# The tail of a hybrid decoder step: where a tile's transposes stand among the products, and the order of combining, gating and norms

## The reference

```python
def _rmsnorm(x, g):
    y = x * rsqrt(mean(x * x, axis=-1) + RMS_EPS)
    return y * g

def _post_mixer(h, mix, p_l, w_out_l, norm_ffn_l, ..., norm_ple_l, pgw, ppw):
    h = h + mix @ w_out_l
    h = h + _hier_moe(_rmsnorm(h, norm_ffn_l), ...)      # each token: 2 of 16 experts, weights w1 and w2
    gate = sigmoid(_rmsnorm(h, norm_ple_l) @ pgw)        # pgw: 1024 x 1024
    return h + gate * (p_l @ ppw)

y_prompt = _rmsnorm(hp, norm_final)                      # 512 x 1024
y_sample = _rmsnorm(hs, norm_final)                      # 8 x 1024
```

## Time and profile before

| | us |
|---|---|
| three runs, median | 1059.52 |
| lowest and highest of them | 1059.48, 1064.51 |
| profiled execution, its own time | 1065.51 |
| span from its first to its last instruction | 1063.3 |

### The profile page before, as it was taken

How to read it: one execution, slowest core, us unless ns; L and a number is a source line. 1 busy time by engine, 2 the same in 40 slices (tenths; PEclk the granted TensorE clock), 3 DMA queues, 4 the chain that set the end, 5 groups by cost and what they waited for, 6 DMA issues and landing times.

```text
span 1063.3 us, 15679 instructions
## 1 busy us (share of the span) xinstructions
PE 935.1 (88%) x6393; PEld 495.7 (47%) x6393; DVE 380.2 (36%) x806; ACT 238.3 (22%) x600; POOL 81.6 (8%) x96
## 2 busy tenths in 40 slices
PE   3996999999999999978978997899998978892996
PEld 3453556654547676665435554443333423341442
DVE  3205645562325747354542125221111111112345
ACT  3116212220123223353212112110000000001335
POOL 1000000000004533000000000100000000002100
PEclk9999999997999989978688999899999989997998
DMA  6454233033246662164603606379999999995101
GB/s 208 178 218 178 31 139 139 4 137 142 79 167 221 235 192 82 42 216 139 198 10 114 259 22 256 127 275 347 378 394 401 402 396 388 407 405 208 41 22 61
DMA packets 72099, 208.76 MB, mean 196 GB/s; under 512 B 15937, under 2 KB 48148, under 8 KB 67548
## 3 DMA queue, kind: packets, MB, share of 16 engines
q1 hardware_dynamic: 57344, 184.73, 46.9%
q0 software_dynamic: 3936, 14.22, 4.0%
q10 hardware_dynamic: 10748, 8.80, 2.6%
HBM read 188.31 MB, written 38.25 MB: 213 GB/s over the span
## 4 chain that ended last, share of the span: by engine, by line
PE 71%; DMA 11%; DVE 10%; ACT 4%; issue 2%; SPq 1%; ACTq 0%; POOL 0%; DVEq 0%; POOLq 0%
PE ps L1930 17%; DMA EXPERT<-in_moe_w_up 9%; PE ps L2354 8%; PE ps L1935 8%; PE ps L2240 6%; PE ps L2460 6%; PE ps L2389 3%; PE ps L2363 3%; PE ps L1965 2%; PE ps L2309 2%; PE ps L2011 1%; PE ps L2092 1%; PE ps L2038 1%; PE ps L1939 1%; PE ps L1914 1%
## 5 line engine op out<-in xcount | busy, mean ns | idle before, releaser
L1930 PE MATMUL ps<-xT,EXPERT 128*128 128x512 f32 x384 | 182.1, 619 | 1.2 <-DVE EXPERT L1263 1.2
L2354 PE MATMUL ps<-EXPERT,aF 128*32 128x512 f32 x1024 | 117.3, 611 | 20.5 <-DMA EXPERT<-in_moe_w_up 12.2
L1935 PE MATMUL ps<-EXPERT,xT 128*128 128x384 f32 (+1 forms) x384 | 121.7, 459 | 1.6 <-ACT EXPERT L917 1.6
L1930 PEld LDWEIGHTS ps<-xT,EXPERT 128*128 128x128 f32 x384 | 71.4, 196 | 79.5 <-issue 75.8
L1935 PEld LDWEIGHTS ps<-EXPERT,xT 128*128 128x128 f32 x384 | 78.8, 238 | 24.6 <-issue 3.5
L2354 PEld LDWEIGHTS ps<-EXPERT,aF 128*32 128x32 f32 x1024 | 34.3, 112 | 99.4 <-issue 81.2
L2460 PE MATMUL ps<-EXPERT 128*128 128x512 f32 x128 | 58.7, 618 | 5.3 <-DVE EXPERT L1891 5.3
L2389 PE MATMUL ps<-EXPERT,dF 128*32 128x512 f32 x512 | 58.2, 595 | 3.3 <-ACT dF L1168 3.3
L2240 PE MATMUL ps<-EXPERT,xT 128*128 128x512 f32 x128 | 60.0, 621 | 1.1 <-ACT xT L1087 1.1
L1843 DVE TENSOR_TENSOR dF<-dF,ps 64x512 f32<-64x512 f32 x16 | 11.0, 690 | 138.6 <-ACT dF L1164 138.6
L1164 ACT ACTIVATE dF<-ps 64x512 f32<-64x512 f32 x16 | 9.4, 590 | 207.4 <-PE ps L2354 207.4
(11 more groups left out here) (439 smaller groups left out, 1234.8 us busy)
## 6 DMA issues: line engine op xcount, KB each, us to landing
EXPERT<-in_moe_w_gate SPq DMA_DIRECT2D x16, 2048.0 KB, 15.9
EXPERT<-in_moe_w_up SPq DMA_DIRECT2D x16, 2048.0 KB, 20.9
EXPERT<-in_moe_w_down SPq DMA_DIRECT2D x16, 2048.0 KB, 21.8
EXPERT<-in_w_in SPq DMA_DIRECT2D x13, 1536.0 KB, 6.6
out_win_sample<-in_cache_win SPq DMA_DIRECT2D x16, 1022.0 KB
aF<-in_cache_k_diff SPq DMA_DIRECT2D x32, 192.0 KB, 2.5
aF<-in_cache_v_diff SPq DMA_DIRECT2D x32, 192.0 KB, 2.5
Yd<-wk ACTq DMA_DIRECT2D x34, 128.0 KB, 9.0
```

The source lines that it names most:

```text
L1930: last = t.matmul(ps[:, u % 2, :], W_[:, c, c0:c0 + w], xT[:, c, 0:SEQ], start=(c == 0), stop=(c == DC - 1))
L1935: last = t.matmul(ps[:, u % 2, 0:w], rows_, W_[:, c, c0:c0 + w], start=(c == 0), stop=(c == DC - 1))
L2354: last = t.matmul(ps[32 * q:32 * q + 32, 2, :], xgT[:, c, 32 * (q % 2):32 * (q % 2) + 32], w[:, c, :], start=(c == 0), stop=(c == DC - 1))
```

## The change

On TensorE, the transposes of tile i + 1 move from behind ple(i) to between its two halves. For tile 4, which has no two halves, `ple` returns before that place, and there is no tile 5.

On VectorE, the loop's body becomes two functions, `combine` (steps 2 and 4) and `gate_columns` (step 6), and tile i + 1 is combined right behind the columns of tile i, ahead of the finish of tile i - 1. The last norm of tile i - 2 and the finish of tile i - 1 change places.

On ScalarE, the rms of tile i + 1 stands ahead of the gate of tile i - 1, and the last rms of tile i - 2 ahead of both.

No operation is added or taken away.

```diff
@@ ScalarE
-            for i in range(T5):
+            def tile_rms(i):
                 act.wait_ge(S_["comb_ok"], i + 1)
                 inv_rms(i, "hn_e")
+
+            tile_rms(0)
+            tile_rms(1)
+            for i in range(1, T5):
                 if i >= 2:
                     act.wait_ge(S_["po_ok"], i - 1)
                     inv_rms(i - 2, "n4_e")
-                if i:
-                    gate(i - 1)
-                    s.preload_act_table_set("natural_log_exp_and_others")
+                if i < NT:
+                    tile_rms(i + 1)
+                gate(i - 1)
+                s.preload_act_table_set("natural_log_exp_and_others")
             gate(NT)
@@ VectorE
-            for i in range(T5):
+            def combine(i):
+
                 r = tile_rows(i)
                 dve.wait_ge(yload[i % 2], 32 * (i // 2 + 1))
...
                 v.tensor_scalar(Ub[i % 3][0:r, :], XM[0:r, i, :], rstd[0:r, i:i + 1], None,
                                 ALU.mult).then_inc(S_["hn_ok"], 1)
+
+            def gate_columns(i):
+
+                r = tile_rows(i)
                 dve.wait_ge(S_["hnt_pe"], i + 1)
                 if i >= 2:
                     dve.wait_ge(S_["pg_pe"], i - 1)
...
                                 f2(gains[:, 16:24], r), ALU.mult).then_inc(S_["hnt_ok"], 1)
+
+            combine(0)
+            for i in range(T5):
+                gate_columns(i)
+                if i < NT:
+                    combine(i + 1)
+                if i >= 2:
+                    last_norm(i - 2)
                 if i:
                     finish(i - 1)
-                if i >= 2:
-                    last_norm(i - 2)
             finish(NT)
@@ TensorE, ple(i)
                 for hf in range(2):
+                    if hf:
+                        columns(i + 1)
                     for c in range(DC):
                         last = t.matmul(ps[0:r, 4 + 2 * (i % 2) + hf, :], hnT[i % 2][:, c, 0:r],
                                         ple_[:, c, hf * 512:(hf + 1) * 512], start=(c == 0), stop=(c == DC - 1))
@@ TensorE
             columns(0)
             for i in range(T5):
                 ple(i)
-                if i < NT:
-                    columns(i + 1)
```

## The result

The changed kernel's median is 1054.03 us over 20 runs, the kernel before's in the same comparison 1059.49 us over 20 runs. The ratio is 0.9933, 95% interval [0.9908, 0.9957]: faster by 0.7%, or 1052.4 us (1049.8 to 1055.0) on the scale of the 1059.52 us given before. The ratio of the two medians given here is 0.9948, or 1054.0 us, which lies inside the range.

What follows compares the result with a forecast made beforehand. The prediction took TensorE's chain of products, transposes and VectorE's copy-out to bound the tail. Gains of 1.48, 3.17 and 0.63 us made 5.28, of which 5.2 reach the end: 1059.52 - 5.2 = 1054.3 us, range 1053.0 to 1059.6.

Steps and rivals of the forecast that it cites:

- The mechanism: TensorE's gate products in the tail: transposes between product halves hide the copy-out; about 5.2 us reach the end.
- The four waits: TensorE's idle time ahead of tiles 1 to 3 and the sample product: 1.31, 1.32, 1.32 and 0.46 us would go.
- the period: TensorE, one tile's products to the next's: 14.61 us in place of 16.20, priced from the w_out stage.
- Tile 3 with the small transposes: TensorE, tile 3 up to the sample product: 14.43 us in place of 15.06, 0.63 us gained.
- ScalarE's table at the end: ScalarE, sample tile's sigmoid: table in 3.81 us after the sample product's start, last by about 0.1 us.
- the scatter: Whole-kernel time: half a microsecond or so allowed around gains of 5.41 to 4.41 us.
- B: Whole-kernel median: the time doesn't show, since runs lie 5.0 us apart outside the tail; 1059.3 us, chance 18%.
- A: Gate products: only the idle time goes, pieces start up as now; 4.4 us, 1055.1 us, within the forecast's 73%.
- C: Middle of products: VectorE and ScalarE become the bound, transposes wait for scaled rows; no change, 1059.5 us, chance 4%.
- D: Middle of tiles 0 to 3: the clock falls at the transposes; 12.9 us, 1067.2 us, 0.7% slower, chance 5%.
- D's price for a fall: Middle of a tile's products: 2.54 us for six slow passes and 0.90 us for eight transposes, 3.4 us.

Runs made afterwards that it cites:

- after_again: The changed kernel, unedited, measured again against the kernel before: ratio 0.9968 [0.9943, 0.9992], tail 80.11 us.
- after_third: The changed kernel, unedited, measured once more against the kernel before: ratio 0.9946 [0.9908, 0.9985], tail 80.07 us.
- late4: The changed kernel with four useless VectorE operations (4.63 us) ahead of the scaling of tiles 2 to 4: tail 79.96 us, at full clock 77.10.
- pe_only: The kernel before with TensorE's part of the change alone, VectorE and ScalarE in the old order: ratio 1.0055 [1.0020, 1.0090], tail 89.87 us.
- late8: The changed kernel with eight useless VectorE operations (9.30 us) ahead of the scaling of tiles 2 to 4: tail 88.58 us.
- before: The kernel before the change, as first profiled: tail 84.85 us, profiled execution 1065.51 us.
- aa: The kernel before, unedited, against itself: ratio 1.0013 [0.9986, 1.0039], tail 83.85 us.
- ve_only: The changed kernel with TensorE's old order, so VectorE's and ScalarE's part alone: ratio 1.0003 [0.9975, 1.0030] to the kernel before, tail 85.24 us.
- warm_before: The kernel before with 20 useless TensorE products around the wait ahead of tile 0: ratio 1.0001 [0.9965, 1.0036], tail 81.30 us.
- warm_again: The changed kernel with 16 useless TensorE products in the wait ahead of tile 0, second measurement: ratio 0.9925 [0.9892, 0.9957] to the kernel before, tail 77.93 us.
- warm_table: The changed kernel with 16 useless products ahead of tile 0, without ScalarE's two table changes between the sigmoids of tiles 3 and 4: ratio 0.9974, tail 77.83 us.
- warm: The changed kernel with 16 useless TensorE products in the wait ahead of tile 0: ratio 0.9933 [0.9905, 0.9961] to the kernel before, tail 76.23 us.

## Why the prediction was right or wrong

**The mechanism was right.** The four waits are gone, the copy-out runs beside the second half, no new wait stands in a product, and the tail at full clock is 5.1 us shorter, where 5.2 were forecast. Its terms: the period, 14.61 forecast from the earlier trace rows, 14.61 measured. Tile 3 with the small transposes was put too low: from its start to the sample product 14.43 us forecast, and 6.96 + 0.59 + 7.06 = 14.61 measured (1020.90 - 1007.07 - 6.87, 1021.49 - 1020.90, 1028.55 - 1021.49), so 0.18 us less gained. ScalarE's table at the end, taken as 0.09 us late, is just in time, so 0.09 us more gained: tile 3's sigmoid starts 1028.66 - 1028.55 = 0.11 us after the sample product, where 0.20 was taken. Together they make 5.1 us out of the 5.2.

**The step that failed is the scatter**: the term "half a microsecond or so" around the forecast, and with it the low end of the range, 1053.0. No row gave that term, and it goes against the prediction's own remark that some 5.3 us can't be told from no change. I had three runs, read two that agreed within 0.04 us as a stable median, and gave the 5 us of the third a rival of its own, on the slow side only. The 20 runs of the kernel before show 1053.96 to 1069.95 us, with a standard deviation of 4.8 us, and the unedited kernel against itself came out at 1.0013 with an interval of 0.27% on either side, 2.8 us. A ratio of 0.9933 for an effect of 0.9952 is within that. The point lay outside the range because the range gave the fast side 1.3 us and the scatter needs more than twice that. That it fell outside is chance as far as the runs show: the medians of the same runs put it at 1054.0 us, `after_again` at 1056.1 and `after_third` at 1053.8, all inside. B was the right cause with the wrong form: the scatter lies mostly outside the tail, as it said (without products in the wait ahead, the low clock at tile 0 adds 1.6 to 3.1 us inside it), but it works both ways.

**A** (only the idle time goes) is out by the period of 14.61, **C** by the 7.3 us that the scaled rows are ahead (7.4 forecast) and by `late4`, which took 4.6 of them without a wait. **D**, the clock's fall at the transposes, didn't come: the granted clock is 1.00 from the first transposes in the middle to the sample product, over 50 us. The rule weighed there, that the full clock does not engage in transposes (the Trainium skill, *TensorE: Matmul & The Clock Gate*, Part 4), isn't borne out here: eight transposes take 1.94 us where the granted clock is 0.50 and 1.04 to 1.06 where it is 1.00. That is for transposes with products around them; what transposes alone do to the clock no run shows. D's price for a fall, 3.4 us (2.5 of it for the products), was too high for the falls that did come in the middle of products, behind waits in `pe_only` and `late8`: they cost 1.7 us each (8.83 - 7.13 and 15.60 - 13.90).

The prediction gave 54% to a difference within 0.5% and 41% to faster by more than that. The first comparison is on the faster side, and all three together, 0.50%, lie on the border.

## What to carry to other kernels

Where an engine waits at every tile for another engine to carry its own result over, put that result's producer half a tile earlier in its list, and then check that the other lists feed it in time: here each half of the edit alone gains nothing or loses. Price such a move from a place in the same trace where the same sequence already runs. And before a gain of half a percent is forecast, ask how far the kernel lies from itself; compare a stage's length in the traces, with the clock's share taken out, where whole runs can't tell.

## What the runs showed of the hardware

- The run time of this kernel scatters by 5 us (standard deviation) without any edit, mostly in the stretch of the mixers, which took 139.7 to 150.1 us in five profiles of two kernels, at granted clocks of 0.88 to 0.80.
- Idle times of 1.31 us between the full products of the tail left the clock at 1.00 in all four profiles with TensorE's old order (`before`, `aa`, `ve_only`, `warm_before`), as did waits of 1.81 and 3.01 us in the middle of products in `pe_only` and of 1.96 and 2.50 us in `late8`. It fell behind a wait of 2.97 us in `pe_only` and of 3.08 us in `late8`. After the useless products, it fell with 0.81 and 1.32 us of idle time around eight transposes in `warm_again` and `warm_table` and not in `warm`.
- A switch of ScalarE's table takes 1.28 us, and a sigmoid of 1.02 us with two switches behind it was just hidden by the sample product of 3.7 us.
